# Two transformer blocks on one core: norm squares paired on GpSimd, routing reordered, opening reordered

## The reference

```
hx = adaln(x, norm1_g, shift, scale)              # rmsnorm(x, g) * (1 + scale) + shift
x  = x + gate * token_mixing(hx, hc, ...)         # window attention + mLSTM, then w_out
hx = adaln(x, norm2_g, ...)
x  = x + gate * channel_mix(hx, ...)              # layer 0: swiglu; layer 1: 8 experts, top 2
def moe_swiglu(h, w_router, b_router, w1, w3, w2):
    logits = t @ w_router + b_router
    top_v, top_i = lax.top_k(logits, 2); top_w = softmax(top_v)
    combine = sum(one_hot(top_i, 8) * top_w)
    y = sum over e of combine[:, e] * swiglu(t, w1[e], w3[e], w2[e])
```

## Time and profile before

| | us |
|---|---|
| median of 3 runs (lowest, highest) | 2670.54 (2667.34, 2671.54) |
| profiled execution, its own time | 2673.33 |
| its span | 2671.5 |
| PE busy | 2513.2 (94%) |
| DVE busy | 1814.5 (68%) |
| ACT busy | 1312.6 (49%) |
| POOL busy | 29.6 (1%) |
| mean granted TensorE clock | 0.955 |

### The profile page before, as it was taken

How to read it: one execution, slowest core, us unless ns; L and a number is a source line. 1 busy time by engine, 2 the same in 40 slices (tenths; PEclk the granted TensorE clock), 3 DMA queues, 4 the chain that set the end, 5 groups by cost and what they waited for, 6 DMA issues and landing times.

```text
span 2671.5 us, 33651 instructions
## 1 busy us (share of the span) xinstructions
PE 2513.2 (94%) x13358; PEld 2053.7 (77%) x13358; DVE 1814.5 (68%) x2870; ACT 1312.6 (49%) x1981; POOL 29.6 (1%) x29
## 2 busy tenths in 40 slices
PE   6999998999998989899999999999898999998998
PEld 3464657788776658688788887888798899988998
DVE  4778626676431434699899898898867675576774
ACT  2135513222222343577677776787644554444553
POOL 0000000000000000000000000000000000000000
PEclk8999998999998989899999999999999899998999
DMA  7522023555321102498898897898843345432552
GB/s 287 189 109 96 1 79 111 189 203 190 125 79 48 64 32 80 184 353 340 309 366 325 324 368 292 325 366 328 310 143 125 111 174 201 146 128 109 176 188 95
DMA packets 71675, 512.06 MB, mean 192 GB/s; under 512 B 7904, under 2 KB 9056, under 8 KB 10048
## 3 DMA queue, kind: packets, MB, share of 16 engines
q1 hardware_dynamic: 68688, 500.20, 50.2%
q10 hardware_dynamic: 2208, 7.37, 0.7%
q0 software_dynamic: 592, 1.97, 0.2%
HBM read 507.27 MB, written 2.23 MB: 191 GB/s over the span
## 4 chain that ended last, share of the span: by engine, by line
PE 83%; DVE 9%; ACT 6%; issue 1%; DMA 1%; DVEq 0%; ACTq 0%
PE bank L767 81%; DVE UL L1892 1%; ACT UH L1433 1%; DVE arena L1900 1%; DVE arena L1892 1%; ACT arena L1436 1%; ACT HT L1436 1%; DMA XT<-in_x 1%; PE bank L1076 1%; DVE HGl L1892 1%; DVE HT L1892 1%; ACT L1436 1%; DVE JUNK L1939 0%; DVE arena L1896 0%; DVE small L1959 0%
## 5 line engine op out<-in xcount | busy, mean ns | idle before, releaser
L1892 DVE TENSOR_TENSOR UL<-ring,UH 128x1024 fp32r<-128x1024 f32 x738 | 886.0, 1212 | 213.6 <-ACT UH L1433 194.3
L1433 ACT CAST UH<-ring 128x1024 fp32r<-128x1024 f32 x738 | 761.4, 1039 | 352.7 <-PE bank L767 344.5
L767 PE MATMUL bank<-XH,UH 128*128 128x256 f32 x1040 | 308.9, 297 | 9.6 <-DVE XL L1892 8.3
L767 PE MATMUL bank<-UH,HGh 128*128 128x512 f32 (+1 forms) x768 | 292.8, 381 | 17.9 <-DVE HT L1892 6.6
L767 PE MATMUL bank<-XL,UH 128*128 128x256 f32 x1040 | 297.6, 286 | 0.0
L767 PE MATMUL bank<-XH,UL 128*128 128x256 f32 x1040 | 297.3, 286 | 0.0
L767 PE MATMUL bank<-UH,HGl 128*128 128x512 f32 (+1 forms) x768 | 289.9, 377 | 0.0
L767 PE MATMUL bank<-UL,HGh 128*128 128x512 f32 (+1 forms) x768 | 288.9, 376 | 0.0
L1433 ACT CAST UH0a<-ring 128x1024 fp32r<-128x1024 f32 x66 | 69.0, 1048 | 324.1 <-PE bank L767 318.7
L767 PEld LDWEIGHTS bank<-XH,UH 128*128 128x128 f32 x1040 | 201.8, 194 | 22.0 <-issue 15.5
L1939 DVE CUSTOM_DVE_ANT_0 JUNK<-ring,CROW 128x1024 bf16<-128x1024 f32 x176 | 206.0, 1218 | 17.8 <-ACT CROW L1436 17.1
(11 more groups left out here) (210 smaller groups left out, 4380.9 us busy)
## 6 DMA issues: line engine op xcount, KB each, us to landing
ring<-in_w SPq DMA_DIRECT2D x477, 1024.0 KB, 4.8
XT<-in_x ACTq DMA_DIRECT2D x1, 2048.0 KB, 20.2
bias_scratch<-BIAS POOLq DMA_DIRECT2D x6, 192.0 KB, 2.1
consts<-in_c ACTq DMA_DIRECT2D x1, 1109.0 KB, 8.0
CROW<-in_r ACTq DMA_DIRECT2D x1, 1024.0 KB, 13.3
out_y<-XT ACTq DMA_DIRECT2D x2, 512.0 KB, 3.5
BIAS<-bias_scratch POOLq DMA_DIRECT2D x1, 768.0 KB, 7.9
constd<-in_c ACTq DMA_DIRECT2D x1, 768.0 KB, 4.2
```

The lines of the kernel that those rows point to most:

```text
L767: return e.matmul(out, lhsT, rhs, start=start, stop=stop, skip_group_check=True)
L1433: return e.copy(out, in_)
L1892: return e.tensor_tensor(out, a, b, op)
```

## The change

1. **Squares in pairs.** The squares get four buffers instead of two (eight at the opening, where they are written into H), and GpSimd adds square k+1 to square k in place (`pairs`). `moments` then runs over the 4 (2) pair sums rather than 8 (4) squares. All places named above.
2. **Opening.** CROW is loaded ahead of params and constants. PE does rows 0 and rows 1 in a row, then moments, turned and spread. The waits for the second constants move from the opening to the first users (`gate`, `rope` 0), and the staging place of the masks moves off Q's memory.
3. **Routing.** The logits are made as 8 rows (8 matmuls with the router's columns as weights, 256 columns of H as data), evicted by DVE, and turned by two small matmuls after half of the token transposes. DVE converts one unit instead of three ahead of the logits; after the selection it forms the low parts, places, counts and PK, and only then the softmax weights and the other two units.
4. **Counts.** `value_load` of one count instead of eight: expert 0's before it, each next one behind the end of the body before.

```diff
-    out.append(("first_stats",))
+    out.append(("first_squares",))
     out.append(("rows", 1, [(("rows", 1, k), "w_mod", (0,), [(128 * k, 1536, 512)]) for k in range(8)]))
     pump(4)
-    out.append(("first_norm",))
+    out.append(("first_stats",))
     out.append(("turned",))
+    out.append(("first_root",))
...
+        def expert_size(e, e_):
+            return e.value_load(CNT[0:1, e_:e_ + 1], min_val=0, max_val=256)
...
             def moments(tile, nblk, nt, src):
                 b = take(w, tile)
-                for k in range(nblk):
-                    w.wait_ge(*act.at("square", tile, k))
+                for k in range(0, nblk, 2):
+                    w.wait_ge(*pool.at("pair", tile, k))
...
-                tile = ("logits",)
-                b = take(w, tile)
-                for tb in range(2):
-                    for k in range(8):
-                        w.wait_ge(*act.at("n2", 1, k))
-                        m = mm(b[:, 8 * tb:8 * tb + 8], H[:, k, 256 + 128 * tb:384 + 128 * tb], wr[:, k, :], k == 0, k == 7)
-                m.then_inc(*sums.up(tile))
+                rows = take(w, ("logit rows",))
+                for k in range(8):
+                    w.wait_ge(*act.at("n2", 1, k))
+                    m = mm(rows[0:8, 0:256], wr[:, k, :], H[:, k, 256:512], k == 0, k == 7)
+                m.then_inc(*sums.up(("logit rows",)))
...
+                        if (tb, hf) == (0, 1):
+                            b = take(w, ("logits",))
+                            w.wait_ge(*vec.at("logit rows"))
+                            for t in range(2):
+                                m = mm(b[:, 8 * t:8 * t + 8], LT[:, 128 * t:128 * t + 128], con("I", 0, 8, 8), True, True)
...
-                    w.wait_ge(s_load[2], 16)
-                    w.wait_ge(s_load[3], 16)
...
                 elif kind == "sized":
                     two_ways(e, w, [sums], [], counts[l] > 128, lambda wide: sized(st[2], wide))
+                    if l < 7:
+                        counts.append(expert_size(e, l + 1))
...
-                elif kind == "first_stats":
-                    tile = ("stat", 0, "n1g")
-                    w.wait_ge(s_load[2], 16)
-                    squares(tile, lambda k: X[:, k, :], SQ1, 512, 8, lambda k: (s_load[2], 16))
-                    root(tile, 4)
+                elif kind == "first_squares":
+                    squares(("stat", 0, "n1g"), lambda k: X[:, k, :], H, 512, 8, lambda k: (s_load[2], 16), bufs=8)
+                elif kind == "first_root":
+                    root(("stat", 0, "n1g"), 4)
...
-            def squares(tile, src, SQ, n, nblk, ready, before=None):
+            def squares(tile, src, SQ, n, nblk, ready, before=None, bufs=4):
                 for k in range(nblk):
                     w.wait_ge(*ready(k))
-                    if k >= 2:
-                        w.wait_ge(*sums.at("moment", tile, k - 2))
+                    if k >= bufs:
+                        w.wait_ge(*sums.at("moment", tile, k // 2 * 2 - bufs))
...
+            load(5, CROW[:, :].rearrange("p (c k) -> p c k", c=2), r_in.unsqueeze(0).to_broadcast([128, 2, 1024]))
             load(0, PR[:, :], p_in)
             load(1, CS[:, 0:1024], c_in[:, 0:1024])
-            load(5, CROW[:, :].rearrange("p (c k) -> p c k", c=2), r_in.unsqueeze(0).to_broadcast([128, 2, 1024]))
             load(2, XT[:, :], x_in)
             w.wait_ge(s_load[0], 16)
             w.wait_ge(s_load[1], 16)
...
                 elif kind == "rope":
                     m = st[2]
+                    if (l, m) == (0, 0):
+                        w.wait_ge(s_load[3], 16)
+                        w.wait_ge(s_load[6], 16)
+                        w.wait_ge(s_load[4], 16)
+                        e.tensor_copy(CB[:, :], bstage).then_inc(*vec.up(("masks",)))
...
+            def pairs(tile, SQ, n, nblk, bufs=4):
+                for k in range(0, nblk, 2):
+                    w.wait_ge(*act.at("square", tile, k + 1))
+                    sq = SQ[:, k % bufs, 0:n]
+                    e.tensor_tensor(sq, sq, SQ[:, (k + 1) % bufs, 0:n], ALU.add).then_inc(*pool.up(("pair", tile, k)))
```

More of the change, by code:

```diff
@@ L1019, in route @@
                 give(("places",))
-                w.wait_ge(*vec.at("counts"))
-                return [e.value_load(CNT[0:1, i:i + 1], min_val=0, max_val=256) for i in range(8)]
             def pick(e_):
@@ L1375, in tensor_program @@
                 elif kind == "route":
-                    counts = route()
+                    route()
+                    w.wait_ge(*vec.at("counts"))
+                    counts.append(expert_size(e, 0))
                     pick(0)
@@ L2196, in route @@
                 tt(wv[:, :, 0:1], v2[:, :, 0:1], v1[:, :, 0:1], ALU.subtract).then_inc(*vec.up(("gap",)))
+                for tb in range(2):
+                    for hf in range(2):
+                        w.wait_ge(*act.at("htok", tb, hf))
+                        low = HTl[:, 4 * tb + 2 * hf:4 * tb + 2 * hf + 2, 0:256]
+                        tt(low, psum(("htok", tb, hf))[:, :].rearrange("p (b c) -> p b c", b=2),
+                           HTh[:, tb, 512 * hf:512 * hf + 512].bitcast(F32).rearrange("p (b c) -> p b c", b=2),
+                           ALU.subtract).then_inc(*vec.up(("htok", tb, hf), free=[("htok", tb, hf)]))
+                w.wait_ge(*sums.at("places"))
+                tt(pos, psum(("places",))[:, 0:16].rearrange("p (t e) -> p t e", e=8), sel,
+                   ALU.mult).then_inc(*vec.up(("pos0",)))
+                w.wait_ge(*vec.now())
+                ts(pos, pos, -1.0, None, ALU.add).then_inc(*vec.up(("pos",)))
+                e.tensor_copy(CNT[0:1, :], psum(("places",))[0:1, 16:24]).then_inc(*vec.up(("counts",), free=[("places",)]))
+                one_hot(0)
                 w.wait_ge(*act.at("ratio"))
@@ L2227, in route @@
                     *vec.up(("tw",)))
+                split_low(W.first["route"], UNITS)
                 picked(0)
-                return found
+                counts.append(expert_size(e, 0))
             def halves(wide, fn):
```

88 lines of the change are left out of this document (44 added, 44 removed).

## The result

The changed kernel takes 2652.95 us (median of 4 runs, 2649.27 to 2653.34), the kernel before beside it 2671.04. The ratio is 0.9927, with a 95% interval of 0.9911 to 0.9943: faster by 19.5 us (18.1 by the two medians). The forecast was 2648.8 us, 21.7 us less than before. The profiled execution has a span of 2651.1 us, where before had 2671.5.

A forecast was written before the change was run, and what follows sets the result against it. PE was taken as the bound, 83% of the chain that ended last. Terms -6.5 - 4.3 - 2.0 - 1.8 - 1.2 - 10.2 + 4.3 = -21.7 us gave 2648.8 us by the median, range 2639 to 2661.

The forecast's parts named there:

- The opening, -6.5 taken: Start of the kernel: projections begin at about 46.2 us instead of 53.47, a gain of 7.3, taken as 6.5.
- Removed is the wait for the second constants: In the opening: PE's wait of 5.57 us for constants leaves, while loads, rows 1 and moments only move.
- The pair sums: GpSimd sums, 1.3 us per 512 columns, shorten statistics: FFN -4.3, layer 1's mix -2.0, `second` -1.8, both `memory` stages -1.2.
- `second`: Statistics of 256 columns at the stage `second`: 5.6 us instead of 7.4, a gain of 1.8.
- the port rule: Rival, 0.08: two-input DVE instructions and GpSimd reads of SBUF block each other, at the FFN and `second`; 1.6 us worse, 2650.4.
- The routing, -10.2: Routing: pick begins near 1078.6 us instead of 1088.81, a gain of 10.2 that includes the moments' 2.2.
- On ACT and DVE I take one as hidden: Count loads at experts' ends: hidden on ACT and DVE, which wait for PE to use a unit; uncovered, 0.65 us.
- The loads at the experts' ends, +4.3: Changes of expert: PE's load between two branches adds its whole length, 7 x 0.62 = 4.3 us; 0 if DVE is the limit.
- slower, through the loads: Rival, 0.04: PE's loads at experts' ends cost more; at 3.7 us each no gain, at 4.5 slower by 5.3 us.
- GpSimd's sum twice as long: Rival, 0.13: a pair sum takes 2.6 us, the statistics lose 11 us in all, and the time is 2660.
- The opening gives nothing: Rival, 0.13: late constants and ring slots 4 to 7 asked for later eat the opening's gain; 2655 us.
- The routing gives more: Rival, 0.10: a shorter stop keeps PE at 2.4 GHz in pick, 3 us less; with free loads at experts' ends, 2643.

The follow-up runs named there:

- the run with the moments ahead: The changed kernel with the opening's moments, spread and root ahead of rows 1 again, first normalisation behind DVE's last eight pump passes: 2660.74 us, ratio 0.9956.
- the second pair: Later traces of the same two kernels, before and changed, on two different chips; the changed kernel is 24.2 us ahead at the end of the span.
- the variants with PE's counts moved: The changed kernel with all eight PE counts loaded in the routing: ahead of pick 2644.19 us, or behind pick and ahead of expert 0's branch 2647.43 us.
- scale rows third: The changed kernel with CROW third again in ACT's load order: 2653.30 us, ratio 0.9917; also with single squares in the opening: 2657.43 us, one run.

## Why the prediction was right, and where it was not

The time lies 4.15 us above the forecast and inside the range, and the sign came true. The likeliest case, within 4 us of the sum, is missed by a hair by the median; by the ratio the gain is 19.5 us, 2.2 short of the 21.7. The sum is better than some of its terms, in part by luck: the loads at the experts' ends came out cheaper than summed for a reason that was not in the text.

**The opening, -6.5 taken, 5.45 measured at the projections.** The start of PE (16.8 forecast, 17.38), rows 1 (34.4, 35.7), and DVE's last eight passes (to 41.6, in the trace to 43.0) each came 0.6 to 1.4 us late, all in the same direction: the ring slots were the weak link, as the text said. The step that failed is the reason. "Removed is the wait for the second constants" reads the releaser in the earlier trace rows as the only one; the run with the moments ahead shows a ring wait of 4.91 us behind it, so that moving the constants alone would, by these two rows, have brought some 0.7 us. "I take each gain as carried through to the end" seems to fail by 2.2 us here, since at memory 0 3.3 us were left; but that is the clock of one pair of traces: from the first projection to memory 0 the first trace of before takes 222.9 us, its second 225.0, and the changed kernel 225.0 and 224.9. In the second pair the projections are 6.6 us ahead, which is the term, and memory 0 6.7.

**The scale rows first.** The forecast that they make PE start 4.9 us late was right (5.4). That this costs nothing was right too, to 1.4 us.

**The pair sums.** The price was right: 1.3 and 0.66 us assumed, 1.26 and 0.72 measured, on the estimate from three streams of a memset; that the engine takes the streams one behind the other is not shown by that. The Trainium skill's 4497 ns for 2048 columns (GPSIMD Engine Reference, section 3.1) agrees: 1.24 us for 512 and 0.71 for 256, in rows of two, make 0.18 us and 0.53 for each 256 columns, and so an estimate of 4.4 us for 2048. My estimate from it by plain proportion, 1.1 us, left the fixed part out. FFN -4.3 became -3.5, layer 1's mix -2.0 became -1.5, memory -1.2 became -1.9. `second` was the miss: -1.8 taken, -0.6 measured. Its first sum stands beside DVE's UL and takes 1.51 us instead of 0.72, and so the first moments wait 0.8 us more. That is the port rule, which I had given 0.08 as a rival with up to 1.0 us at this place; its mechanism is real, and my main case should have held it. The other 0.4 us of this miss are open; PE's passes at half the clock are not the reason, since the term had them. At the FFN it costs 0.37 us, less than the 0.6 taken.

**The routing, -10.2 with 2.2 for its moments.** Measured from memory 1 to pick: 11.15 us. The chain is as worked out: DVE's low parts, place, count, one load. From pick to expert 0 it takes 8.96 us instead of 8.38. The cover for the weights and two units was long enough: DVE's last HGl follows ACT's cast at once, as before. What is new is DVE's own load of expert 0's count, which the code puts between HGl and the copy of the slots' weights that SCx and PE wait for. DVE, changed kernel:

```profile
1071.69 0.69 DVE L1904 TENSOR_TENSOR HGl<-bank,HGh 128x512 fp32r<-128x512 f32 x1 [0.26 <-ACT HGh L1446]
1073.22 0.16 DVE L1968 COPY slots<-bank 128x4 f32<-128x4 f32 x1 [0.83 <-issue]
```

These 0.83 us are nowhere in before, and they stand in the second trace and in the variants with PE's counts moved too. "On ACT and DVE I take one as hidden" holds for the seven at the experts' ends and not for this one. Without it expert 0 would have begun sooner behind pick than before (8.13 us), since pick's own passes took 0.46 us less, on the clock.

**The loads at the experts' ends, +4.3.** The net is +1.9 and -0.4 us in the two pairs of traces, so the term was too dear by 2.4 to 4.7 us, and its working was wrong both ways. I took a stop of before as the 1.40 to 1.77 us of the four rows that the trace has whole, and added 0.62 to each. Two errors lie in it. The other three changes of expert were not looked at, and two of them stop for 3.2 and 4.6 us; the changed kernel lacks these, which gives back 4.5 us. And a load costs more than its length: 0.95 us of stop, and in three or four of seven cases a fall of the clock for 1.7 to 3.5 us more. Against a kernel without them the seven loads on PE cost 12.5 to 14.6 us. The rival "slower, through the loads" was therefore nearer than its chance of 0.04 said: 1.8 to 2.1 us a load, and it needed 3.7 (at its 4.5 the sum is 5.5 us slower, not the 5.3 that I wrote). Why before's two changes are so long is open. The Trainium skill (Runtime: NRT & Kernel Launch, "Instruction fetch mechanics") says that a taken branch to code that isn't at hand must wait for its fetch; no run here shows whether that is it, only that the place is fixed in the program and that the wait is charged to nothing.

**The rivals.** "GpSimd's sum twice as long" is out by its row. "The opening gives nothing" is out at the projections, and at memory 0 too by the second pair. "The routing gives more" named the clock in pick; pick's passes took 0.41 us, half the clock, for the first 4.2 us, where before had 5.3, so of its 3 us only 0.5 came, though the same effect was to be had at the experts.

## What to carry to other kernels

Count a repeated stop at all its places, not at those that the timeline prints whole; the length of a stretch minus PE's busy time in it shows what is missing. Loads of registers on the bound engine belong together in one place: eight in a row cost 0.64 us each, at a loop's end one cost three times that. On engines that the bound one does not wait for they were free; on DVE ahead of expert 0, where PE waits for DVE, one cost 0.83 us. Look at a second trace of both kernels before a term is called right or wrong by 2 us. A wait's releaser is the last to come, not the only one: ask what would be waited for next, as the ring was behind the constants.

## What the runs showed of the hardware

- Over all fourteen traces (both kernels twice, ten variants) PE's clock fell to 1.2 GHz, mostly for 3.4 us, in or behind 31 of 61 stops between experts that were over 2 us long, and behind 2 of 37 shorter ones. Which of the longer ones it follows changed between two traces of one kernel. The stops themselves repeat to 0.5 us.
- A sum with two SBUF inputs on GpSimd and a DVE pass with two SBUF inputs slow each other down: 1.22 to 2.28 us for the pass, 4.97 to 7.72 for four sums (scale rows third, with and without the sums).
- A ring load of 1 MB landed in 4.7 us by itself and in 7.4 us beside the load of the second constants (changed kernel at 57.23, before at 45.32).
- Eight loads of a register one behind the other on PE cost 0.64 us each, and none of it was hidden by a wait of PE for another engine's data that stood behind them.
